# Norm factors of the second block: row sums by products of split squares with ones, roots on all 128 partitions by Ln and Exp

## The reference

```
q, k = rms_norm(q, q_gain), rms_norm(k, k_gain)      # per head, over its 128 columns
z    = q k^T / sqrt(128)                             # stick-breaking attention
later[t,s] = sum over s<j<t of log_sigmoid(-z[t,j])
w    = exp(log_sigmoid(z) + later), only for s < t
oa   = (w v) * silu(z_gate)
o    = retention(rotary(q_r), rotary(k_r), v_r)      # per head
ob   = (o - mean(o)) * rsqrt(var(o) + 1e-6) * gain * silu(z_gate)
x    = x + gate * (concat(oa, ob) @ w_out)
```

## Time and profile before

| | us |
|---|---|
| median of 3 runs (2839.41 to 2841.28) | 2840.24 |
| profiled execution | 2841.77 |
| its span in the trace | 2839.6 |
| PE busy | 2790.4 (98%) |
| DVE busy | 1482.9 (52%) |
| ACT busy | 1018.6 (36%) |
| POOL busy | 361.4 (13%) |

### The profile page before, as it was taken

The page is one execution under the profiler, slowest core; times in us unless marked ns, Lnnn a source line. Parts: engine busy times, 40 slices in busy tenths (PEclk is TensorE's granted clock), DMA queues, the critical chain, the costliest instruction groups (busy, mean ns, idle before and its releaser), DMA issues.

```text
span 2839.6 us, 33641 instructions
## 1 busy us (share of the span) xinstructions
PE 2790.4 (98%) x13414; PEld 2271.2 (80%) x13414; DVE 1482.9 (52%) x1763; ACT 1018.6 (36%) x1332; POOL 361.4 (13%) x417
## 2 busy tenths in 40 slices
PE   6999999999999999999999999899999999999999
PEld 2678888888878887888888888688888888788887
DVE  6867768764565456666652333533333333423543
ACT  7742222234343332433332332433343343222311
POOL 1011100001333223331310000100000000000000
PEclk8999999999999999999999999899999999999999
DMA  9647767654545554555454432332222223223342
GB/s 398 233 171 267 256 244 270 248 192 146 171 154 169 157 176 137 168 172 167 150 187 181 137 105 89 126 111 75 75 82 77 78 82 100 83 85 99 109 164 96
DMA packets 162122, 439.37 MB, mean 155 GB/s; under 512 B 14768, under 2 KB 59824, under 8 KB 151728
## 3 DMA queue, kind: packets, MB, share of 16 engines
q1 hardware_dynamic: 123360, 307.28, 33.1%
q0 software_dynamic: 15792, 92.99, 9.2%
q10 hardware_dynamic: 22816, 36.97, 3.6%
HBM read 398.11 MB, written 39.06 MB: 154 GB/s over the span
## 4 chain that ended last, share of the span: by engine, by line
PE 87%; DVE 4%; DMA 1%; issue 1%; ACT 1%; POOL 0%; ACTq 0%; SPq 0%; DVEq 0%; POOLq 0%
PE PB L404 15%; PE PB L410 15%; PE PB L409 15%; PE PB L515 10%; PE PB L517 10%; PE PB L516 10%; DMA AU<-in_w_ada 1%; PE PB L632 1%; PE PB L408 1%; PE PB L407 1%; PE PB L412 1%; PE PB L649 1%; DVE ca L1588 1%; PE PB L883 1%; DVE AACC L1588 1%
## 5 line engine op out<-in xcount | busy, mean ns | idle before, releaser
L1580 DVE TENSOR_TENSOR WL<-RAW,WH 128x1024 fp32r<-128x1024 f32 (+1 forms) x424 | 515.9, 1224 | 796.0 <-ACT WH L992 590.2
L404 PE MATMUL PB<-HH,WH 128*128 128x512 f32 x2048 | 818.0, 399 | 4.7 <-ACT zp L992 1.8
L410 PE MATMUL PB<-HH,WL 128*128 128x512 f32 x2048 | 802.1, 392 | 0.0
L409 PE MATMUL PB<-HL,WH 128*128 128x512 f32 x2048 | 801.1, 391 | 0.0
L992 ACT ACTIVATE WH<-RAW 128x1024 fp32r<-128x1024 f32 (+1 forms) x424 | 433.0, 1038 | 506.3 <-PE PB L517 277.3
L515 PE MATMUL PB<-WH,HH 128*128 128x512 f32 x1248 | 491.7, 394 | 0.0
L517 PE MATMUL PB<-WH,HL 128*128 128x512 f32 x1248 | 486.2, 390 | 0.0
L516 PE MATMUL PB<-WL,HH 128*128 128x512 f32 x1248 | 485.9, 389 | 0.0
L404 PEld LDWEIGHTS PB<-HH,WH 128*128 128x128 f32 x2048 | 385.1, 188 | 94.3 <-issue 11.0
L410 PEld LDWEIGHTS PB<-HH,WL 128*128 128x128 f32 x2048 | 386.0, 188 | 67.1
L409 PEld LDWEIGHTS PB<-HL,WH 128*128 128x128 f32 x2048 | 386.5, 189 | 64.7 <-issue 3.1
(11 more groups left out here) (302 smaller groups left out, 2688.8 us busy)
## 6 DMA issues: line engine op xcount, KB each, us to landing
RAW<-in_w_in_t SPq DMA_DIRECT2D x320, 512.0 KB, 3.6
AU<-in_w_ada POOLq DMA_DIRECT2D x64, 1024.0 KB, 5.6
RAW<-in_w_out_t SPq DMA_DIRECT2D x96, 512.0 KB, 3.5
bcb<-R SPq DMA_DIRECT2D x64, 256.0 KB, 6.1
S<-so ACTq DMA_DIRECT2D x24, 384.0 KB, 2.6
ebc<-R SPq DMA_DIRECT2D x32, 256.0 KB, 5.3
SY<-evb ACTq DMA_DIRECT2D x32, 256.0 KB, 2.5
yin<-SY POOLq DMA_DIRECT2D x32, 256.0 KB, 4.2
```

What stands on the lines that cost most here:

```text
L404: h.matmul(banks[j], lh, m.HH[:, t, :], start=st, stop=False)
L409: h.matmul(banks[j], lh, m.HL[:, t, :], start=False, stop=False)
L410: ins = h.matmul(banks[j], ll, m.HH[:, t, :], start=False, stop=en)
L1580: return h.tensor_tensor(o, a, b, op)
```

## The change

The sums of squares come from products with a 128x128 matrix of ones that is already there rounded (`m.exact["ones"]`), so that each of the 128 partitions gets the sum for all 512 tokens. For that the square is split: ACT writes it twice, in full (SHs) and rounded (SHh), and DVE subtracts (SHl). Two products a tile (high, low) give the sum in a bank. ACT takes Ln, then Exp with scale -0.5, which is the root; DVE multiplies with it, and a refining step follows: with r the root and a = -0.5*mean - 0.5*EPS (Identity on ACT), the tile is multiplied with 1.5 + a*r*r (Square on ACT, two instructions on DVE). POOL's loop of `power`, with its waits for "rc", and the transposes are gone. SHr lies where SHh lay and SHs where SHl lay, in 8 KB that nothing used in this phase.

Tiles 0 and 1 (q) of a pair are now squared and summed within the pair's own k projection (squares behind `make` of its unit 12, the products within unit 13 in the banks that q's projection used, `roots` on ACT and `norm` on DVE behind `make` of unit 14, before that unit's piece), tiles 2 and 3 (k) in pieces 0 to 2 as before. In retention the products lie within the unit after the piece that gives o of head 1, and `roots` and `normalise` one piece after it; the last step is one unit earlier than before. On POOL the load of g2 no longer stands behind the power of pair 7, and the first load of xq waits for "normed", 7, 1, because xq lies over the SH buffers.

```diff
+    def row_sums(p, tiles, held=None):          # TensorE, in place of col_rms and spread
+        for j in tiles:
+            if held:
+                b = m.bank["sums", p, j] = held[j]
+                bank = reuse(b)
+            else:
+                b, bank = take(hb, "sums", p, j)
+            P.wait_ge(*at("exact"))
+            P.wait_ge(*at("square high", p, j))
+            h.matmul(bank, m.exact["ones"], m.SHh[:, j % 2, :], start=True, stop=False)
+            yield
+            P.wait_ge(*at("square low", p, j))
+            h.matmul(bank, m.exact["ones"], m.SHl[:, j % 2, :], start=False, stop=True) \
+                .then_inc(*put(P.side, "sums", p, j))
+            drop(main if held else hb, b, ("log", p, j))
+            if j != tiles[-1]:
+                yield
...
     def project(u0, p, name):                    # TensorE
         for k4 in range(4):
             t_unit(u0 + k4, k4, [tk[0][1], tk[1][1]], second_h)
+            if name == "k" and p < 4 and k4 == 0:
+                fine.append(row_sums(p, (0, 1), held))
+            if k4 == 1:
+                drain(fine)
...
+    def square(src, p, j):                       # ScalarE
...
+        A.then(act(m.SHs[:, j % 2, :], src, ACT.Square), "square", p, j)
+        A.then(act(m.SHh[:, j % 2, :], src, ACT.Square), "square high", p, j)
...
+    def roots(p, tiles):
+        A.wait_ge(*at("eps"))
+        for j in tiles:
+            A.wait_ge(*at("sums", p, j))
+            A.then(act(m.SHs[:, j % 2, :], bank("sums", p, j), ACT.Identity, scale=-0.5 / 128, bias=m.epsh))
+            A.then(act(m.SHr[:, j % 2, :], bank("sums", p, j), ACT.Ln, scale=1.0 / 128, bias=m.epsc), "log", p, j)
+        for j in tiles:
+            A.wait_ge(*at("log", p, j))
+            A.then(act(m.SHr[:, j % 2, :], m.SHr[:, j % 2, :], ACT.Exp, scale=-0.5), "root", p, j)
+        for j in tiles:
+            A.wait_ge(*at("rooted", p, j))
+            A.then(act(m.SHr[:, j % 2, :], m.SHr[:, j % 2, :], ACT.Square), "root squared", p, j)
...
+            if p is not None and k4 == 0:
+                square_tile(p, 0)
+                square_tile(p, 1)
+            if p is not None and k4 == 2:
+                roots(p, (0, 1))
             step(bg)
...
+    def square_low(p, tiles):                    # VectorE
...
+            V.then(TT(m.SHl[:, j % 2, :], m.SHs[:, j % 2, :], m.SHh[:, j % 2, :].bitcast(F32), ALU.subtract),
+                   "square low", p, j)
...
+    def normalise(xs, p):
+        for j, x, gain in xs:
+            V.wait_ge(*at("root", p, j))
+            V.then(STT(x, x, gain, m.SHr[:, j % 2, :], ALU.mult, ALU.mult), "rooted", p, j)
+        for j, x, gain in xs:
+            V.wait_ge(*at("root squared", p, j))
+            t = V.then(TT(m.SHs[:, j % 2, :], m.SHs[:, j % 2, :], m.SHr[:, j % 2, :], ALU.mult))
+            V.wait_ge(*t)
+            V.then(STT(x, m.SHs[:, j % 2, :], 1.5, x, ALU.add, ALU.mult), "normed", p, j)
...
+            if p < 4 and k4 == 14:
+                norm(p, (0, 1))
             step(bg)
+            if p < 4 and k4 == 12:
+                square_low(p, (0, 1))
...
-    for p in range(8):                           # GpSimd
-        G.wait_ge(*at("rc", p))
-        N = 4 if p < 4 else 2
-        power(m.rc[:, 0:4 * N], "rc power", p)
-    for e in ("y2", 13), ("normed", 6, 1), ("gates out", 3, 2), ("gates out", 3, 3):
+    for e in ("y2", 13), ("gates out", 3, 2), ("gates out", 3, 3):
         G.wait_ge(*at(*e))
     load(m.g2, m.GT[1], s.g2, "g2")
+    G.wait_ge(*at("normed", 7, 1))
```

More of the change, by code:

```diff
@@ L217, in memory @@
     m.ss2, m.xsq, m.A2 = sm(24), sm(8), sm(16)
-    m.rc, m.vm, m.qgs, m.onec = sm(16), sm(8), sm(1), sm(1)
+    m.vm, m.qgs, m.onec, m.epsc, m.epsh = sm(8), sm(1), sm(1), sm(1), sm(1)
     m.scv = m.sc.rearrange("p (t j) -> p t j", j=2)
@@ L333, in memory @@
             lst.append(x)
-        o += (1 - i) * 8 * KB
+        if i == 0:
+            m.SHr = at("SHr", o, [128, 2, 512])
+            m.SHh, o = mem("SHh", [128, 2, 512], o, F32R)
+            m.SHl = at("SHl", o, [128, 2, 512], F32R)
+            m.SHs, o = mem("SHs", [128, 2, 512], o)
     m.Vr, o = mem("Vr", [128, 4, 512], o)
@@ L824, in second_h @@
         P.wait_ge(*at("HL2", t))
-    def col_rms(p, sq, N, *key):
-        b, bank = take(hb, "rms", p)
-        if N == 2:
-            yield
[L830 to L847, removed]
+    def row_sums(p, tiles, held=None):
[8 more added lines that the diff above has]
+            h.matmul(bank, m.exact["ones"], m.SHh[:, j % 2, :], start=True, stop=False)
+            yield
+            P.wait_ge(*at("square low", p, j))
[4 more added lines that the diff above has]
+                yield
     def stick(p):
@@ L851, in stick @@
         tiles = [m.Qr[i][:, 0, :], m.Qr[i][:, 1, :], m.Kr[i][:, 0, :], m.Kr[i][:, 1, :]]
-        sq = [m.LN[:, 0:512], m.LN[:, 512:1024], m.E1[:, 0:512], m.E1[:, 512:1024]]
-        fine.append(col_rms(p, sq, 4, "squared", p))
+        fine.append(row_sums(p, (2, 3)))
         yield
@@ L856, in stick @@
         yield
-        for j in range(4):
-            spread(p, j, ("normed", p, j))
         yield
@@ L924, in retain @@
             drop(hb, b, ("ob", hd))
-        fine.append(col_rms(p, [m.LN[:, 0:512], m.LN[:, 512:1024]], 2, "squared", p))
+        fine.append(row_sums(p, (0, 1)))
         yield
         drain(fine)
-        yield
-        for hh in range(2):
-            spread(p, hh, ("normed", p, hh))
     main, hb = deque([0, 1, 2, 3]), deque([4, 5, 6, 7])
@@ L935, in tensor_program @@
     bg = deque([m2])
+    held = {}
     def project(u0, p, name):
@@ L940, in project @@
             t_unit(u0 + k4, k4, [tk[0][1], tk[1][1]], second_h)
+            if name == "k" and p < 4 and k4 == 0:
+                fine.append(row_sums(p, (0, 1), held))
+            if k4 == 1:
+                drain(fine)
             step(bg)
         for e in range(2):
-            drop(main, tk[e][0], ("proj", p, name, e))
+            if name == "q" and p < 4:
+                held[e] = tk[e][0]
+                freed[held[e]] = [("proj", p, name, e)]
+            else:
+                drop(main, tk[e][0], ("proj", p, name, e))
     def heads(p):
@@ L1411, in e_free, with square_tile @@
             A.wait_ge(*at("y2", 2 * p - 1))
-            A.wait_ge(*at("rms", p - 1))
-    def stick(p):
[L1415 to L1421, removed]
+    def square(src, p, j):
+        if p == 0 and j < 2:
+            A.wait_ge(*at("HL2", 15))
+        elif p > 4:
+            A.wait_ge(*at("normed", p - 1, j))
+        else:
+            A.wait_ge(*at(*(("normed", p - 1, j + 2) if j < 2 else ("normed", p, j - 2))))
+        A.then(act(m.SHs[:, j % 2, :], src, ACT.Square), "square", p, j)
+        A.then(act(m.SHh[:, j % 2, :], src, ACT.Square), "square high", p, j)
+    def square_tile(p, j):
+        A.wait_ge(*at("proj", p, "qk"[j // 2], j % 2))
+        square((m.Qr if j < 2 else m.Kr)[p % 2][:, j % 2, :], p, j)
+    def roots(p, tiles):
[10 more added lines that the diff above has]
+            A.then(act(m.SHr[:, j % 2, :], m.SHr[:, j % 2, :], ACT.Square), "root squared", p, j)
+    def stick(p):
+        square_tile(p, 2)
+        square_tile(p, 3)
         yield
         yield
+        roots(p, (2, 3))
         yield
@@ L1426, in stick @@
             hd = 2 * p + hh
-            A.wait_ge(*(at("av", hd - 1) if hh else at("rms", p)))
+            if hh:
+                A.wait_ge(*at("av", hd - 1))
+            else:
+                e_free(p)
             for sb in range(4):
@@ L1474, in retain @@
         for j in range(2):
[L1475 to L1478, removed]
+            A.wait_ge(*at("ob", 2 * (p - 4) + j))
+            square(m.E1[:, j * 512:(j + 1) * 512], p, j)
         yield
-        yield
+        roots(p, (0, 1))
     m2 = modulate2()
@@ L1487, in scalar_program, with units @@
     bg = deque([m2])
-    def units(u0, n):
+    def units(u0, n, p=None):
         for k4 in range(n):
@@ L1493, in units @@
                 turn_output(t)
+            if p is not None and k4 == 0:
+                square_tile(p, 0)
+                square_tile(p, 1)
+            if p is not None and k4 == 2:
+                roots(p, (0, 1))
             step(bg)
     def project(u0, p, name):
-        units(u0, 4)
+        units(u0, 4, p if name == "k" and p < 4 else None)
         if p < 2:
@@ L2038, in vector_program @@
     V.then(h.memset(m.onec, 1.0), "one")
+    V.then(h.memset(m.epsc, EPS))
+    V.then(h.memset(m.epsh, -0.5 * EPS), "eps")
     take_out(0)
@@ L2079, in modulate2, with norm @@
                 yield
[L2081 to L2085, removed]
+    def square_low(p, tiles):
+        for j in tiles:
+            V.wait_ge(*at("square", p, j))
+            V.wait_ge(*at("square high", p, j))
+            V.then(TT(m.SHl[:, j % 2, :], m.SHs[:, j % 2, :], m.SHh[:, j % 2, :].bitcast(F32), ALU.subtract),
[9 more added lines that the diff above has]
```

(20 more changed lines are left out.)

## The result

| | before | after |
|---|---|---|
| median of 5 runs each, us | 2841.28 (2839.41 to 2842.44) | 2827.43 (2824.31 to 2827.6) |
| ratio | | 0.9949 (95% interval 0.9935 to 0.9964) |
| profiled execution, us | 2841.77 | 2824.31 |
| its span | 2839.6 | 2822.5 |

The forecast was 2822.0 with a range of 2817 to 2832, and for the profiled execution 2823.6 with a span of 2821.4. The same kernel, run five times more in a second set, gave 2823.74 against 2844.01 for the kernel before: ratio 0.9933 (0.992 to 0.9945). So the kernel is 14 to 20 us faster, by which set one takes; experiment 1 looks for a cause of such scatter. One of the five runs of experiment 3 took 3978.24 us at a mean granted clock of 0.653; the median given there counts it, the ratios are of the fast runs alone.

A forecast was written before the change was run, and what follows sets the result against it. PE, busy 98% of the span, was taken as the bound: 33.0 us leave its stream, 10.9 come, waits cost 3.9, so 18.2 us less. From the median of 2840.24 that gave 2822.0 us, range 2817 to 2832.

The forecast's parts named there:

- 33.0 us less of sums and transposes: On PE, four pairs each in attention and retention lose the old sums and transposes, 5.50 and 2.74 us a pair.
- 10.9 us for 48 products: On PE, two new 128x512 products a tile at 0.2277 us each; upper bound 0.1 more each, 4.8 us.
- The waits: PE waits 2.2 us before tile 0's low product, 0.6 before `av`, 1.1 before first output block's unit 7: 3.9.
- ACT's work: ACT gets 6 instructions a tile instead of 1, about 76 us, costing nothing by itself since ACT has room.
- The chain: From L, the start of a pair's last sum product, to both tiles normed on ACT and DVE: 8.0 us.
- Retention's slack of 0.7: In p = 4, 5, 6 DVE's weights are ready at L + 10.4, PE needs them at L + 11.1: no wait.
- xq: Its load goes out at 2694.1, lands 8.0 to 9.7 us later, holds DVE up to 4 us; PE loses nothing.
- Rival (b): Chains behind the last sum come out 2 us longer, 12 us more of waits: 2834 us; chance 0.15.
- (c): A table switch holds ACT 2.7 us instead of 1.3, 7.7 us more: 2830 us; chance 0.03.
- (d): New waits in p = 1, 2, 3 and 7 make the clock fall, 8.4 us each: 2856 us; chance 0.06.
- (e): PE isn't relieved: weight halves come late and its waits eat the 18 us won: 2840 us; chance 0.06.
- (a): The time comes as worked out, 2822 us, own range 2818 to 2827 for waits of 0 to 8.5; chance 0.70.

The follow-up runs named there:

- experiment 1: The changed kernel again, no edit, for a second profile and more runs: second block's eleventh unit to last product (the stretch) 924.73 us, against 924.64 in the first profile.
- experiment 3: Against the changed kernel, VectorE makes the low halves for t = 14 and 15 before unit 8's weight half in the first output block: stretch 923.65 us, ratio 0.994.
- experiment 5: Against the changed kernel, a third product added to each of the 24 row sums, right behind the second: stretch 930.13 us, 5.4 to 5.5 more.
- experiment 4: Against the changed kernel, the refining step left out (96 instructions on ACT and DVE): stretch 923.15 us, 1.5 less; 2823.9 us, ratio 0.9932.
- experiment 6: Against the changed kernel, late first sums, low halves for t = 14, 15 before unit 8's weight half, w's mask before a weight half: stretch 921.01 us, ratio 0.9926.
- experiment 2: Against the changed kernel, the sums of tiles 0 and 1 start six products later: stretch 924.06 us, 0.6 less; 2826.62 us, ratio 0.9943.
- experiment 7: Against the changed kernel, all four products of a pair of tiles stand together at the unit's end, in twelve places: stretch 932.69 us, 8.0 more.
- experiment 8: Against the changed kernel, 14 idle VectorE fills before the low parts of tiles 0 and 1 in p = 1, 2, 3: stretch 947.16 us, 22.5 more.

## Why the prediction was right, and where its terms were off

- **PE is the bound, and what leaves its stream is won.** Shown: experiment 5 adds its products' time, and experiments 4, 5 and 6 move the stretch by what they move on PE or in front of it.
- **33.0 us less of sums and transposes.** Held. 33.0 - 10.9 - 1.9 - 3.4 = 16.8 by the terms below; the stretch gained 16.70.
- **10.9 us for 48 products.** Too small by 1.9 us, a mis-sized term: a lone product costs 0.268 to 0.28 us, not 0.228. The measured 12.8 lie within the stated bounds. In p = 0, where nothing waits, the eight of them left a gain of 3.36 us where 5.50 - 1.82 = 3.68 was worked out. "No surcharge for that matrix" was right of a product next to its like; the surcharge lies mostly in the neighbours, which rows of one product's length couldn't show, and 0.1 for the event, the upper bound, was too much.
- **The waits.** Forecast 0.4, 1.4, 0.4, then 0.2 three times, then 1.1: 3.9. Measured 0.28, 1.24, 0.28, with 0.1 each for the restart; 0.07 three times before `av` and once before `z` in p = 7; 0.96 and 0.07 before unit 7: 3.4. Experiments 3 and 6 remove them where the prediction put them; experiment 2 moves most of them. This term, 0.5 too large, made good a part of the 1.9: the stretch gained 16.70 where 18.2 was forecast, and the profiled execution 17.5; the rest of that lies outside the stretch.
- **ACT's work.** 94.5 us against 76: the sum left out 18 more table loads of 1.28 us each. It cost nothing.
- **The chain.** L + 7.9 against L + 8.0. Retention's slack of 0.7: no wait there in the changed kernel, as forecast, and experiment 7 uses it up.
- **xq.** Issued at 2677.97, landed 5.7 us later, first read at 2684.28, with no wait of PE in the second output block. That this costs nothing was forecast; but DVE wasn't held at all, where up to 4 us were allowed for.
- **Rival (b)**, longer chains, and **(c)**, the drain, fall by the rows above: by the Trainium skill ("ScalarE: Activation LUTs", What ACT_TABLE_LOAD costs) each switch would take 2.7 us; the trace shows 1.29. **(d)** falls for this change: the clock is 1.00 in both windows and behind its longest wait. But its condition is nearer than experiment 8 alone would say, with a fall behind a single gap of 3.31 us in experiment 7, and its price was too high: 1.7 to 2.5 us a fall, not 8.4. The 8.4 came from a place where PE was idle 11.5 us of 30, not the 3.4 named. **(e)** falls by the windows and by experiment 4.
- **The median.** 2827.4 in one set and 2823.7 in the other, for 2822.0 forecast. The profiled execution came at 2824.31 for 2823.6. The first set's median lies just outside the 2818 to 2827 of (a) and inside the values given for (b); that (a) is nevertheless what happened is shown by the waits and the chain in the traces, not by that number. Most of the first set's distance is probably scatter of the first block, but its longer runs have no trace, and why DVE's halves are late there in some executions wasn't followed up.

## What to carry to other kernels

Where one engine is busy all the time, price an edit by stretches with the same number of its instructions, with and without the work in question, and then look only at the order of the others around each new wait. Here each small wait was something needed soon that stood behind something needed late: three steps of reordering gave back 3.6 us, about all that the waits had cost. A wait that grows can cost more than its length: look at the granted clock behind it before you put a loss down to the wait alone. And a wait taken away at one place (experiment 2) or work put together for tidiness (experiment 7) lengthens a chain elsewhere; work out which part of it had lain ahead of the last input.

## What the runs showed of the hardware

- A lone 128x512 product with the matrix of ones among a steady stream stretches the starts around it from 0.227 to 0.228 to 0.237 us, seven of them, 0.04 us in all. A group of four has about the same surplus once (experiment 7), and a second product right behind one costs 0.227 (experiment 5).
- Gaps of TensorE of about 6 us brought the granted clock to 1.2 GHz for about 6.7 us and cost 1.7 to 2.5 us besides (experiment 8). One of 3.31 us brought it down for 3.4 us and cost some 1.7 (experiment 7). Single ones of up to 2.18 us, start to start, left it at 1.00 in the second block.
- Of kernels that are the same in the first block, two profiled executions came to its end 5.4 us later than a third, by waits for weight halves at 560 to 575 us and a fall of the clock behind them.
